# Attention loop of a two-block layer: a head's twelve units ordered in pairs, and the next head's preparation moved between them

## What is computed

```
for blk in range(S // Q_BLOCK):                  # 8 blocks of 128 queries
    s = einsum(q_blk, k[:, :k_end]) * scale      # head width 96
    s = where(k_chunk <= q_chunk, s, -inf)       # chunks of 64 tokens
    p = softmax(s)
    out = einsum(p, v[:, :k_end])                # v has width 64
```

## Time and profile before

| | us |
|---|---|
| median of 3 executions | 2829.2 |
| lowest, highest | 2828.47, 2833.79 |
| the profiled execution, its own time | 2830.83 |
| its span, first to last instruction | 2829.0 |
| PE busy in the span | 2657.8 (94%) |
| DVE, ACT, POOL busy | 1596.7, 1200.7, 338.1 |
| from S0 of head 0 to V11 of head 15, about | 1946.8 to 2274.3 |

### The profile page before, as it was taken

One profiled execution on the slowest core, in us unless ns is written; L12 is line 12 of the kernel. 1 busy time (PEld: TensorE's weight loads), 2 busy tenths in 40 slices (PEclk: granted clock), 3 DMA queues, 4 the chain that ended last, 5 costly groups with the idle time before them and its releaser, 6 DMA issues. The chain is left out here.

```text
span 2829.0 us, 32119 instructions
## 1 busy us (share of the span) xinstructions
PE 2657.8 (94%) x12144; PEld 2094.4 (74%) x12144; DVE 1596.7 (56%) x2120; ACT 1200.7 (42%) x1743; POOL 338.1 (12%) x289
## 2 busy tenths in 40 slices
PE   6999999999999999999999989899999879599993
PEld 5888888888878787777777779897666658477772
DVE  5688888888641323443343333686666543666664
ACT  4234444344340213545235323564555521366661
POOL 0010111101100000000000000133122210342213
PEclk9999999999999999999999999999999989699997
DMA  5333323333245212021121131234322031999997
GB/s 188 112 123 108 108 75 108 108 108 101 75 146 196 78 49 82 30 75 43 55 74 42 49 134 34 88 120 164 113 60 56 13 92 68 364 356 347 355 353 275
DMA packets 209160, 362.65 MB, mean 128 GB/s; under 512 B 51911, under 2 KB 159816, under 8 KB 195320
## 3 DMA queue, kind: packets, MB, share of 16 engines
q1 hardware_dynamic: 193432, 322.94, 33.0%
q0 software_dynamic: 14720, 34.64, 3.2%
q10 hardware_dynamic: 864, 3.15, 0.3%
HBM read 310.72 MB, written 116.93 MB: 151 GB/s over the span
## 5 line engine op out<-in xcount | busy, mean ns | idle before, releaser
L398 PE MATMUL PS<-UHI,WHI 128*128 128x512 f32 x1008 | 415.8, 413 | 4.1 <-DVE ULO L127 4.1
L398 PE MATMUL PS<-ULO,WHI 128*128 128x512 f32 x1008 | 400.2, 397 | 0.0
L398 PE MATMUL PS<-UHI,WLO 128*128 128x512 f32 x1008 | 400.2, 397 | 0.0
L127 DVE TENSOR_TENSOR WLO<-arena,WHI 128x1024 fp32r<-128x1024 f32 x94 | 115.3, 1227 | 215.7 <-ACT WHI L123 215.6
L398 PEld LDWEIGHTS PS<-UHI,WHI 128*128 128x128 f32 x1008 | 190.6, 189 | 52.3 <-issue 5.5
L398 PEld LDWEIGHTS PS<-ULO,WHI 128*128 128x128 f32 x1008 | 190.6, 189 | 47.6 <-issue 5.5
L398 PEld LDWEIGHTS PS<-UHI,WLO 128*128 128x128 f32 x1008 | 190.2, 189 | 46.3
L1500 PE MATMUL PS<-U2HI,WHI 128*128 128x512 f32 x480 | 193.0, 402 | 2.7 <-DVE WLO L127 2.7
L1500 PE MATMUL PS<-U2HI,WLO 128*128 128x512 f32 x480 | 189.4, 395 | 0.0
L1500 PE MATMUL PS<-U2LO,WHI 128*128 128x512 f32 x480 | 189.4, 395 | 0.0
L834 DVE SCALAR_TENSOR_TENSOR RC<-arena,cols,RC 128x1024 f32<-128x1024 f32 x120 | 157.2, 1310 | 10.3 <-issue 0.9
(11 more groups left out here) (465 smaller groups left out, 6019.4 us busy)
## 6 DMA issues: line engine op xcount, KB each, us to landing
arena<-in_w_in SPq DMA_DIRECT2D x88, 512.0 KB, 3.9
xd_dram<-in_x SPq DMA_DIRECT2D x32, 768.0 KB, 6.9
y_dram<-in_x SPq DMA_DIRECT2D x32, 768.0 KB, 6.8
arena<-in_w_gate SPq DMA_DIRECT2D x13, 1024.0 KB
arena<-in_w_up SPq DMA_DIRECT2D x13, 1024.0 KB
arena<-in_w_down SPq DMA_DIRECT2D x13, 1024.0 KB, 13.7
qk_dram<-RA SPq DMA_DIRECT2D x32, 384.0 KB, 2.3
arena<-qk_dram SPq DMA_DIRECT2D x32, 384.0 KB, 4.4
```

The source lines that it names most:

```text
L127: return eng.tensor_tensor(dst, src, hi.bitcast(F32), ALU.subtract)
L398: last = pe.matmul(o[:, h * HALF:(h + 1) * HALF], x[:, k, :], y[:, k, h * HALF:(h + 1) * HALF], start=(k == r == 0), stop=(k == ND - 1 and ...
```

## The change

PE takes the units of a head in twos. For b = 0 to 5 it issues S(2b), S(2b+1), then work for other heads, then V(2b), V(2b+1). The trial products of the next head go to b = 0 (T0, T1, T2), b = 1 (T3, T4), b = 2 (T5, T6) and b = 3 (T7). `turn_tops` goes to b = 4, the two turns to b = 4 and b = 5. On ACT, `tops_hi` moves from after E7 to after E9, and the two `features_hi` from after E8 and E9 to after E9 and E11. The number and the sizes of all instructions stay.

```diff
+        TRIALS = ((0, 1, 2), (3, 4), (5, 6), (7,), (), ())
...
                 for h in range(NHEADS):
-                    scores(h, 0)
-                    scores(h, 1)
-                    for k in range(NUNIT):
-                        if k + 2 < NUNIT:
-                            scores(h, k + 2)
+                    for b in range(NUNIT // 2):
+                        scores(h, 2 * b)
+                        scores(h, 2 * b + 1)
                         if h + 1 < NHEADS:
-                            if k < 4:
-                                trial(h + 1, 2 * k)
-                                trial(h + 1, 2 * k + 1)
-                            if k == 6:
+                            for i in TRIALS[b]:
+                                trial(h + 1, i)
+                            if b == 4:
                                 turn_tops(h + 1)
-                        if h + 2 < NHEADS and 7 <= k < 9:
-                            turn_head(h + 2, k - 7)
-                        values(h, k)
+                        if h + 2 < NHEADS and b >= 4:
+                            turn_head(h + 2, b - 4)
+                        values(h, 2 * b)
+                        values(h, 2 * b + 1)
...
-                        if k == 7 and h + 1 < NHEADS:
+                        if k == 9 and h + 1 < NHEADS:
                             tops_hi(h + 1)
-                        if 8 <= k < 10 and h + 2 < NHEADS:
-                            features_hi(h + 2, k - 8)
+                        if k in (9, 11) and h + 2 < NHEADS:
+                            features_hi(h + 2, (k - 9) // 2)
```

## The result

| | before | after |
|---|---|---|
| median, us | 2829.29 | 2842.2 |
| lowest, highest of 5 | 2828.47, 2833.79 | 2839.24, 2846.26 |
| profiled execution, its span | 2830.83, 2829.0 | 2839.24, 2837.4 |
| heads 1 to 13, from S0 to S0 | 258.50 | 265.63 |

The lines of the loop stand one further down than before on PE (S is L1724, V L1737, T L1704, the turns L1693) and one further up on ACT, DVE and POOL (E is L1981 and L1983, `results` L1990, `features_lo` L2380, the maximum L2391, the reciprocals L2401, the merge L2076 to L2080).

The account below looks back on a forecast made before the run. PE was taken to set the length of a head, through its stream and stalls. Heads 1 to 13 (7.3), head 0 (0.3) and heads 14 and 15 (6.4) gave 14.0 us: 2829.2 + 14.0 = 2843.2 us, range 2828 to 2854.

Parts of the forecast that it names:

- The twos save nothing in the stream: PE's stream over all heads: the same matmuls run and type changes cost no stream time, so a saving of 0.
- b = 0: V0 starts at 2.91 instead of 1.62, behind the late features_lo chain and T0's maximum: 1.29 us lost.
- b = 3: V7 waits for E7, which ACT runs after results: 0.65 us lost, and b = 3 lasts 4.25.
- b = 4, 5: V8 to V11 without stall; the turn covers E10 and E11, so the 0.39 us of before goes.
- POOL: Reciprocals of even heads release the merge late, putting the next head's V2 at 5.80, not 5.68: 0.12 us in seven heads.
- Heads 1 to 13: Middle heads together: 13 x (20.39 - 19.88) + 7 x 0.12 = 7.5 us slower, less 0.2, entered as 7.3.
- Head 0: First head: its end has the 0.65 loss but not the 0.39 gain, 0.3 us slower.
- Heads 14 and 15: End of stage: tops_hi behind two splits makes the restart 5.35 us later, plus 0.9 after it: 6.4, +-1.5.
- The sum: Whole kernel: 7.3 + 0.3 + 6.4 = 14.0 us slower, a median of 2843.2.
- (a): Rival: type changes cost stream time, at most 0.40 us each, 64 fewer in 16 heads: 2817.6 at that bound; chance 0.12.
- (b): Rival: the chain to V0 is no bound, second features_lo ends by 1.2, V0 starts at 2.33: 2834.4; chance 0.13.
- (c): Rival: late steps at E0, V0 and V2 push one another, 0.7 us more a head, 9 us: 2852; chance 0.15.

Follow-up runs that it names:

- E7: Not a run: an exponential on ACT, which V7 waits for.
- E11: Not a run: an exponential on ACT, which V11 waits for.
- E10: Not a run: an exponential on ACT, which V10 waits for.
- E2: Not a run: an exponential on ACT, which V2 waits for.

## Why the prediction was right, and where it was not

**The twos save nothing in the stream: right.** V4 to S6 above, and 56 added pairs of changes at 0.9997. The argument from the rows was weaker than it looked. The 0.855 for a V was itself got as 1.09 less 0.235, across a change of type, so a cost of the change would have been inside it, and V4 to V5 would have added up all the same. The two V in a row of the kernel after part the two. The Trainium skill, FP8 and Floating Point Precision, section TensorE Precision Notes, gives true fp32 four passes. The 0.853 us for a full V that I estimated from it fits the 0.855 of both kernels, with nothing over for a change.

**b = 0: right.** V0 came at 2.91 into head 4 (2.79 into head 5), predicted 2.91. Its cause, the chain from `turn_tops` (15.61 into the head; predicted 15.7) through four DVE steps to T1, is in the rows. The kernel with V0 first shows that 2.91 could be 1.69; the kernel with `turn_tops` earlier, that the prediction named only one of two limbs. It was right on the number since the other limb ends at most about 0.1 us earlier: in that kernel V0 still comes at 2.78 into head 4. That the limb left out was not the longer one is luck.

**b = 1, 2: right.** No stall of PE in the timeline between V0 and V7.

**b = 3: right.** It lasts 4.21 (predicted 4.25), from the stream of S6 at 2039.73 to that of S8 at 2043.94. With `results` behind E7 the wait is gone, for 0.72 a head: it was worth more than its own 0.65.

**b = 4, 5: right.** No stall. The kernel with both turns in b = 4 shows that the turn in b = 5 was the cover of E10, as laid out.

**POOL: right in place, too small.** Odd heads were to be 0.12 longer; they are 0.24 longer (20.57 against 20.33). I had laid V2 at 5.80 by a sum of four durations, where a tenth counts.

**Heads 1 to 13:** predicted 7.3, measured 7.13. Heads of 20.39 and 20.51 were predicted, 20.33 and 20.57 came. The even ones are 0.06 shorter and the odd ones 0.06 longer than laid out, and that this cancels in the sum is luck.

**Head 0: wrong by its whole size.** Predicted +0.3; it took 26.73 in both, at a mean granted clock of 0.81 in both. The wait for E7 is there in the kernel after (0.37). What makes up for it was not taken apart and stays open.

**Heads 14 and 15: mechanism right, one term wrong.** E2 of head 15 was to end 33.35 after head 14's S0 began; it ended after 33.24. After that I added 0.9 for V2, V3, S4 and S5 at the half clock and V4's wait for E4, and this term failed (5.35 and 0.9 are 6.25 besides, not the 6.4 of the sum). From E2 to `results(15, 0)` it is 7.31 now and was 7.53 before. The half clock came for V2, V3, S4 and S5 as laid out, but it went sooner than before: V4 and V5 no longer have it, where S6 and V4 had it before. The stretch after PE's restart, in the kernel before:

```profile
2260.10:2266.30 6.20, 6.17 (x15) 4.61 (x16) 0.00 (x0) 3.28 (x6) 0.00 (x0) 0.50 0.00 0
```

And in the kernel after:

```profile
2267.20:2270.90 3.70, 3.65 (x10) 2.93 (x10) 0.00 (x0) 1.76 (x4) 0.00 (x0) 0.50 0.00 0
```

I had taken for granted that what ran at the half clock before would do so again. From head 14's S0 to the end of the stage it is 57.53 before and 62.53 after: 5.0, not 6.4.

**The sum.** 7.13 + 0 + 5.0 = 12.1 against 14.0. The medians moved 12.9, which holds both within the interval (10.2 to 16.4). The two profiled spans differ only by 8.4, since the stages ahead of this one ran 5.2 shorter in the profiled execution of the kernel after, and those behind it 1.5 longer. They are unchanged, and vary by as much elsewhere: over the profiled executions of all kernels here S0 of head 0 starts between 1940.91 and 1947.13. Read alone, the spans would have called the change cheaper than it is.

**The rivals.** (a) is refuted above. (b), a chain that is no bound: V0 at 2.3 was its mark, and it came at 2.91. (c), steps that push one another by 0.7 a head: not here, heads are where they were laid. The kernel with T2 in b = 1 shows that such a case lay close: 21.04 and 21.16 a head.

## What to carry to other kernels

A wait of the weight loader that the profile calls "issue" was no time of PE here; add up starts across the place before paying for its removal, and take the cost of each part from a place where the other is absent. When work is moved later, follow its results through every engine's queue into the next iteration, and look for the second limb: here the DVE chain, `results` and the merge each had a small remedy, and one remedy bared the next bound. On the changed kernel none alone beat the kernel before (the best came to 1.0006), and together they did. Where two buffers alternate, ask of every group of more than two what returns the first buffer.

## What the runs showed of the hardware

- **Going between fp32r and fp32 matmuls costs PE's stream nothing.** 56 more pairs of changes between fp32r matmuls and fp32 transposes gave 0.9997, and the starts across four changes add up to the 1.23 us of the matmuls alone. For fp32 matmuls of 512 columns, two of them and a change take 1.95 us and one and a change 1.09.
- **A POOL step can be held off by a whole row of DVE operations, or both can be slowed.** In head 14 a step of 1.27 took 5.47 (5.46 in the kernel after) beside four DVE splits that took 4.55, and ended 1.13 after the last of them; it took 1.27 when they waited. In head 15 the same four splits took 7.77 and the three POOL steps beside them 2.03, 2.06 and 2.06. The Trainium skill, SBUF — State Buffer, section SBUF: two separate sides, says that the one that comes first holds the shared ports for its whole instruction. The trace agrees that they hinder each other. But in head 14 POOL waited through four instructions and not one, and in head 15 all seven were through in 7.77, less than the 8.4 that they need one after the other (4.63 + 3 x 1.27). What decides between the two cases stays open.
- **How long the half clock lasts after a restart is not one number.** It was 6.2 us after an idle time of 5.58, 3.7 after 8.18, and 4.25 after 4.00; after 1.42 idle the clock stayed full. The length of the idle time alone does not decide it: with `results` behind E7 PE stood 8.18 too, and was at the half clock for at least 4.1 after it (2258.50 to 2262.60, granted 0.50). What decides it stays open; no run here was made for it.
